# A two-layer encoder trunk in split fp32: embedding rows transposed inside the output projection, their products moved around the router, y split ahead of the next weights

## The reference

```python
x = x + merged @ w_o[i]
h2 = rms_norm(x, g_ffn[i])
logits = (t @ w_router).astype(jnp.float32)            # t = h2, 256 tokens, 8 experts
top_vals, top_idx = lax.top_k(logits, TOP_K)           # TOP_K = 2
w = jax.nn.softmax(top_vals, axis=-1)
...
acc = acc + g_e[:, None] * swiglu(t, wg_e, wu_e, wd_e) # for each expert e
x = x + acc
gate_p = jax.nn.sigmoid(rms_norm(x, g_ple[i]) @ w_ple_gate[i])
x = x + gate_p * (p[i] @ w_ple_up[i])                  # p[i]: 256 x 256
```

## Time and profile before

| | us |
|---|---|
| median of 3 runs | 1717.95 (1717.78 to 1718.05) |
| the profiled execution | 1716.82 |
| its span, first to last instruction | 1714.9 |
| TensorE matmuls busy | 1674.0 (98% of the span) |
| VectorE busy | 1334.2 (78%) |
| ScalarE busy | 1093.1 (64%) |

### The profile page before, as it was taken

One profiled execution on the slowest core, in us unless ns is written; L12 is line 12 of the kernel. 1 busy time (PEld: TensorE's weight loads), 2 busy tenths in 40 slices (PEclk: granted clock), 3 DMA queues, 4 the chain that ended last, 5 costly groups with the idle time before them and its releaser, 6 DMA issues.

```text
span 1714.9 us, 20962 instructions
## 1 busy us (share of the span) xinstructions
PE 1674.0 (98%) x7899; PEld 1389.7 (81%) x7899; DVE 1334.2 (78%) x1093; ACT 1093.1 (64%) x897; POOL 55.5 (3%) x52
## 2 busy tenths in 40 slices
PE   7999899999999998999999999999999999999997
PEld 6888788888778887888888888888888888888886
DVE  6785644545567856788988998999998999889885
ACT  5555344344455553777877877778778778778774
POOL 0100000000001000010000000000000000000000
PEclk9999999999999999899999999999999999999999
DMA  8433555565364335599999999999999999999990
GB/s 307 167 123 123 172 172 192 176 196 192 117 213 147 123 123 184 191 363 374 358 380 366 350 383 353 373 377 347 373 385 341 379 377 347 382 377 347 376 370 25
DMA packets 199549, 472.60 MB, mean 276 GB/s; under 512 B 8592, under 2 KB 11216, under 8 KB 199504
## 3 DMA queue, kind: packets, MB, share of 16 engines
q1 hardware_dynamic: 197936, 466.20, 75.6%
q0 software_dynamic: 1568, 5.77, 1.0%
HBM read 469.84 MB, written 2.10 MB: 275 GB/s over the span
## 4 chain that ended last, share of the span: by engine, by line
PE 86%; DVE 9%; issue 3%; ACT 2%; DMA 0%; SPq 0%; DVEq 0%; ACTq 0%
PE ps L1293 26%; PE ps L1295 26%; PE ps L1294 26%; DVE w_lo L786 5%; PE ps L1298 5%; PE ps L1622 1%; ACT w_hi L530 1%; DVE y_lo L1236 1%; DVE hT_lo L792 0%; ACT hT_hi L546 0%; PE ps L1542 0%; PE ps L1403 0%; ACT inner_hi L697 0%; DVE hT_lo L844 0%; PE ps L1384 0%
## 5 line engine op out<-in xcount | busy, mean ns | idle before, releaser
L786 DVE TENSOR_TENSOR w_lo<-raw,w_hi 128x2048 fp32r<-128x2048 f32 x442 | 1007.6, 2290 | 246.7 <-ACT w_hi L530 242.3
L530 ACT ACTIVATE w_hi<-raw 128x2048 fp32r<-128x2048 f32 x442 | 846.5, 1919 | 374.7 <-PE ps L1295 365.1
L1293 PE MATMUL ps<-w_hi,hT_hi 128*128 128x512 f32 (+1 forms) x1600 | 631.2, 394 | 10.9 <-DVE hT_lo L844 4.6
L1295 PE MATMUL ps<-w_hi,hT_lo 128*128 128x512 f32 (+1 forms) x1600 | 621.8, 389 | 0.0
L1294 PE MATMUL ps<-w_lo,hT_hi 128*128 128x512 f32 (+1 forms) x1600 | 621.2, 388 | 0.0
L1293 PEld LDWEIGHTS ps<-w_hi,hT_hi 128*128 128x128 f32 x1600 | 301.7, 189 | 77.3 <-DVE w_lo L786 6.0
L1295 PEld LDWEIGHTS ps<-w_hi,hT_lo 128*128 128x128 f32 x1600 | 301.4, 188 | 63.0
L1294 PEld LDWEIGHTS ps<-w_lo,hT_hi 128*128 128x128 f32 x1600 | 302.0, 189 | 58.8
L1293 PE MATMUL ps<-w_hi,inner_hi 128*128 128x512 f32 x608 | 240.3, 395 | 1.6 <-DVE inner_lo L792 1.6
L1295 PE MATMUL ps<-w_hi,inner_lo 128*128 128x512 f32 x608 | 237.8, 391 | 0.0
L1294 PE MATMUL ps<-w_lo,inner_hi 128*128 128x512 f32 x608 | 237.8, 391 | 0.0
(11 more groups left out here) (230 smaller groups left out, 776.2 us busy)
## 6 DMA issues: line engine op xcount, KB each, us to landing
raw<-in_w_moe_gate SPq DMA_DIRECT2D x112, 1024.0 KB, 6.9
raw<-in_w_moe_up SPq DMA_DIRECT2D x112, 1024.0 KB, 7.3
raw<-in_w_moe_down SPq DMA_DIRECT2D x112, 1024.0 KB, 6.7
raw<-in_w_in SPq DMA_DIRECT2D x38, 1024.0 KB, 5.6
raw<-in_w_dense_gate SPq DMA_DIRECT2D x14, 1024.0 KB, 5.0
raw<-in_w_dense_up SPq DMA_DIRECT2D x14, 1024.0 KB, 5.1
raw<-in_w_dense_down SPq DMA_DIRECT2D x14, 1024.0 KB, 4.8
raw<-in_w_o SPq DMA_DIRECT2D x8, 1024.0 KB, 4.8
```

Source lines behind the costliest of these rows:

```text
L530: nc.scalar.activation(w_hi[:, n % SLOTS, :], raw[:, n % RAW_SLOTS, :], ACT.Copy).then_inc(high_ready, 1)
L786: nc.vector.tensor_tensor(w_lo[:, n % SLOTS, :], raw[:, n % RAW_SLOTS, :], w_hi[:, n % SLOTS, :].bitcast(F32), ALU.subtract).then_inc(low_ ...
L1293: nc.tensor.matmul(o, x_parts[0][x_cols], parts[0], start=first, stop=False)
L1295: return nc.tensor.matmul(o, x_parts[1][x_cols], parts[0], start=False, stop=last)
```

## The change

The transposes of p for layer 1 move from in front of the router into the output projection, behind its second unit, and write bank 0 instead of bank 7. ScalarE's copy (`take_p`) and VectorE's `split_p` move with them. The whole first token tile of p @ `w_ple_up` is computed ahead of the router and the whole second tile between the router and the place counting; both write banks 4 to 7. The logits go to banks 0 and 1, the places to bank 2, so the router's first matmul now waits until banks 0 and 1 have been read. ScalarE's two copies of the products move forward, and its split of unit MOE + 2 stands ahead of the gathered tokens. VectorE splits unit MOE + 1 ahead of both gathered lows and unit MOE + 2 ahead of `extras`. In the item loop VectorE makes `y_lo` first and then splits units 1 and 2 of the next item, instead of unit 1, `y_lo`, and unit 2 in the next turn.

```diff
--- before.py
+++ after.py
@@ -143,7 +143,8 @@
 
     TASKS = [(0, 0, 8), (1, 0, 4), (1, 4, 4)]
     OUT_PRODUCTS = 5
-    P_BANK = [4, 7]
+    P_BANK = [4, 0]
+    LOGIT_BANK, PLACE_BANK = 0, 2
     OUT_BANK = [2, 2, 6]
     NORM_BANK = [0, 0, 4]
 
@@ -545,9 +546,7 @@
                         act_e.wait_ge(x_transposed, 4 * n + k // 2 + 1)
                     nc.scalar.activation(hT[0][:, k, :], banks(NORM_BANK[n % 3] + k // 2)[:, k % 2 * SEQ:(k % 2 + 1) * SEQ],
                                          ACT.Copy, scale=params[:, gain + k:gain + k + 1]).then_inc(hT_high, 1)
-                if n == 4:
-                    take_p(1)
-                else:
+                if n != 4:
                     keep_up(used, items, END if n == 5 else None)
                 for t in range(1 if n == 4 else 0, TILES):
                     nc.scalar.activation(normed[:, t, :], x[:, t, :], ACT.Square,
@@ -648,6 +647,9 @@
                     act_e.wait_ge(merged_transposed, 4 * layer + g + 1)
                     nc.scalar.activation(hT[0][:, 2 * g:2 * g + 2, :], banks(g).rearrange("p (k t) -> p k t", k=2),
                                          ACT.Copy).then_inc(mergedT_high, 1)
+                if layer:
+                    keep_up(base + WO_AT + 1)
+                    take_p(1)
                 keep_up(base + WO_AT + GATE_UNITS - 1)
 
             def dense():
@@ -669,9 +671,10 @@
                     act_e.wait_ge(ple_up_tile0, 1)
                 else:
                     act_e.wait_ge(units_used, UP1 + 1)
-                nc.scalar.activation(ple_up[:, t, :], banks(2 * t, 2), ACT.Copy).then_inc(ple_up_taken, 1)
+                nc.scalar.activation(ple_up[:, t, :], banks(4 + 2 * t, 2), ACT.Copy).then_inc(ple_up_taken, 1)
 
             def experts():
+                take_ple_up(0)
                 act_e.wait_ge(rstd_ready, 5)
                 for t in range(TILES):
                     act_e.wait_ge(x_gained_ready, t + 1)
@@ -680,15 +683,14 @@
                 act_e.wait_ge(top_ready, 1)
                 for t in range(TILES):
                     nc.scalar.activation(gate_w[:, t, :], gate_w[:, t, :], ACT.Exp, scale=rstd[:, t:t + 1]).then_inc(route_exps, 1)
-                take_ple_up(0)
+                take_ple_up(1)
+                keep_up(MOE)
 
                 for half in range(2):
                     act_e.wait_ge(gathered, half + 1)
                     nc.scalar.activation(hT[0][:, 4 * half:4 * half + 4, 0:P],
                                          banks(GATE + half).rearrange("p (k s) -> p k s", k=4),
                                          ACT.Copy).then_inc(gatheredT_high, 4)
-                take_ple_up(1)
-                keep_up(MOE)
                 act_e.wait_ge(counted, 1)
                 count = act_e.value_load(n_items_i[0:1, 0:1], min_val=EXPERTS, max_val=EXPERTS + EXTRA)
                 with act_e.Fori(0, count) as t:
@@ -1054,6 +1056,9 @@
                     dve.wait_ge(mergedT_high, 4 * layer + g + 1)
                     low(hT, banks(g).rearrange("p (k t) -> p k t", k=2),
                         (slice(None), slice(2 * g, 2 * g + 2))).then_inc(mergedT_ready, 1)
+                if layer:
+                    keep_up(base + WO_AT + 1)
+                    split_p(1)
                 keep_up(base + WO_AT + GATE_UNITS - 1)
                 add_to_x(4, 3 * layer + 1, base + WO_AT + GATE_UNITS)
 
@@ -1091,10 +1096,10 @@
                 e2 = [P, TILES, EXPERTS, EXPERTS]
                 dve.wait_ge(logits_done, 1)
                 for t in range(TILES):
-                    last = nc.vector.tensor_copy(logits[:, t, :], banks(GATE + t)[:, 0:EXPERTS])
+                    last = nc.vector.tensor_copy(logits[:, t, :], banks(LOGIT_BANK + t)[:, 0:EXPERTS])
                 link(last)
                 for t in range(TILES):
-                    last = nc.vector.tensor_tensor(logits[:, t, :], banks(GATE + t)[:, EXPERTS:2 * EXPERTS], logits[:, t, :], ALU.add)
+                    last = nc.vector.tensor_tensor(logits[:, t, :], banks(LOGIT_BANK + t)[:, EXPERTS:2 * EXPERTS], logits[:, t, :], ALU.add)
                 link(last)
                 other = logits[:, :, :].unsqueeze(2).to_broadcast(e2)
                 own = logits[:, :, :].unsqueeze(3).to_broadcast(e2)
@@ -1110,8 +1115,8 @@
                                         ALU.subtract).then_inc(top_ready, 1)
 
                 dve.wait_ge(places_done, 1)
-                place_ps = banks(TRA)[:, 0:TILES * EXPERTS].rearrange("p (t e) -> p t e", t=TILES)
-                count_ps = banks(TRA)[:, TILES * EXPERTS:(TILES + 1) * EXPERTS]
+                place_ps = banks(PLACE_BANK)[:, 0:TILES * EXPERTS].rearrange("p (t e) -> p t e", t=TILES)
+                count_ps = banks(PLACE_BANK)[:, TILES * EXPERTS:(TILES + 1) * EXPERTS]
                 link(nc.vector.scalar_tensor_tensor(place[:, :, :], place_ps, 1.0, chosen[:, :, :], ALU.add, ALU.mult))
                 link(nc.vector.tensor_scalar(item_place[:, :, 0:EXPERTS], place[:, :, :], -1.0, None, ALU.add))
 
@@ -1178,12 +1183,12 @@
 
             def experts():
                 route()
+                keep_up(UP1)
                 gathered_low(0)
-                keep_up(UP1)
                 gathered_low(1)
+                keep_up(MOE)
                 extras()
                 link(take_slots(slot_now, slice(0, 1)))
-                keep_up(MOE - 1)
                 count = dve.value_load(n_items_i[0:1, 0:1], min_val=EXPERTS, max_val=EXPERTS + EXTRA)
                 with dve.Fori(0, count) as t:
                     def actT_low_part(s):
@@ -1229,12 +1234,12 @@
                         dve.wait_ge(gatheredT_high, KD * (t + 1) + 4 * half + 4)
                         low(hT, banks(GATE + half).rearrange("p (k s) -> p k s", k=4),
                             (slice(None), slice(4 * half, 4 * half + 4), slice(0, P))).then_inc(gatheredT_ready, 1)
-                    keep_up(MOE + PER_ITEM - 1, t)
                     for half in range(2):
                         cols = slice(half * BANK, (half + 1) * BANK)
                         dve.wait_ge(item_y_high, t * 2 + half + 1)
                         nc.vector.tensor_tensor(y_lo[:, cols], banks(half), y_hi[:, cols].bitcast(F32),
                                                 ALU.subtract).then_inc(item_y_split, 1)
+                    keep_up(MOE + PER_ITEM, t)
                 for piece in range(4):
                     dve.wait_ge(item_combined, count * 4 + piece + 1)
                     xv = x[:, piece % 2, piece // 2 * BANK:(piece // 2 + 1) * BANK]
@@ -1278,7 +1283,6 @@
             mixer(1)
             gain_x(0)
             norm_low(4, FFN_GAIN + KD)
-            split_p(1)
             gain_x(1)
             embedding(1, experts())
 
@@ -1507,6 +1511,8 @@
                 for u in range(GATE_UNITS):
                     wide_unit(base + WO_AT, u, GATE_UNITS, hT, 4, ready=mergedT_ready, ready_at=4 * layer,
                               tile0_done=out_tile0 if u == GATE_UNITS - 1 else None)
+                    if layer and u == 1:
+                        flip_p(1)
 
             def dense():
                 def down(s):
@@ -1548,26 +1554,28 @@
 
                 for k in k_tiles:
                     for half in range(2):
-                        last = products(banks(2 * t + half), pT, columns(k, t), UP1, D, k, slice(half * BANK, (half + 1) * BANK),
+                        last = products(banks(4 + 2 * t + half), pT, columns(k, t), UP1, D, k, slice(half * BANK, (half + 1) * BANK),
                                         k == 0, k == PLE // P - 1)
                 if k == PLE // P - 1:
                     last.then_inc(ple_up_tile0 if t == 0 else units_used, 1)
 
             def route():
-                flip_p(1)
+                pe.wait_ge(x_updated, 8)
+                ple_up_tile(0)
                 for k in range(KD):
-                    if k % 2 == 0:
+                    if k == 0:
+                        pe.wait_ge(hT_ready, 16 + 2)
+                    elif k >= 4 and k % 2 == 0:
                         pe.wait_ge(hT_ready, 16 + k // 2 + 1)
                     for t in range(TILES):
 
-                        mm(banks(GATE + t)[:, 0:2 * EXPERTS], hT[0][columns(k, t)], router_parts[:, k, :, :], k == 0, False)
-                        last = mm(banks(GATE + t)[:, 0:EXPERTS], hT[1][columns(k, t)], router_parts[:, k, 0, :], False, k == KD - 1)
+                        mm(banks(LOGIT_BANK + t)[:, 0:2 * EXPERTS], hT[0][columns(k, t)], router_parts[:, k, :, :], k == 0, False)
+                        last = mm(banks(LOGIT_BANK + t)[:, 0:EXPERTS], hT[1][columns(k, t)], router_parts[:, k, 0, :], False, k == KD - 1)
                 last.then_inc(logits_done, 1)
-                pe.wait_ge(pT_ready, 2)
-                ple_up_tile(0)
+                ple_up_tile(1)
 
                 pe.wait_ge(chosen_ready, 1)
-                b = banks(TRA)
+                b = banks(PLACE_BANK)
```

(6 more changed lines are left out.)

## The result

The changed kernel takes 1726.22 us (median of 5 runs, 1725.31 to 1727.44) beside 1717.78 us of the kernel before on the same chip (5 runs, 1717.32 to 1718.05). The ratio is 1.0047 with a 95% interval of 1.0035 to 1.0058: slower, by 6.0 to 10.0 us. The forecast was 1726.1 in a range of 1720 to 1730. One run of a later kernel (after_filled) took 5584 us and is left out of that kernel's median. The profiled execution took 1725.31 us around a span of 1723.5; lines have moved by a few, so the products are now L1297, L1298 and L1299, `mm` is L1302, `y_lo` L1240, `w_lo` L788.

The account below looks back on a forecast made before the run. TensorE's matmuls, busy 98% of the span, were taken as the bound, so time moves only with its waits, clock or work. Terms -1.6 + 6.4 + 1.0 + 2.4 = +8.2 us gave median 1726.1, range 1720 to 1730.

Parts of the forecast that it names:

- Part 3: At item boundaries, y_lo first makes unit 1's split late: +0.82 each, 0.92 with later stops, +6.4 us over seven.
- The follow-up: Behind the late unit in each item, ScalarE's later split, table load and silu: 0.1 us taken, bounds 0 and 0.3.
- Rival 3: Boundary order costs nothing, the 0.38 goes at all seven; -3.3 to -6.5 us in all, about 1713; chance 0.08.
- Rival 4: A new wait of 0.5 us or more at every item's first transposes; +11.6 in all, 1729.5; chance 0.10.
- Parts 1 and 2: Transposes of p moved into the output projection (0.5 us cost), products and router reordered: -1.6 us together.
- Rival 1: The clock holds through the router: -4.8 in place of -1.6, +5.0 in all, 1723.0; chance 0.22.
- The clock: Granted clock low after TensorE's idle stretch behind the last item, slowing the last projection: +2.4 us, bounds 0 and 3.5.
- Part 4: Behind the last item: later adds to x (+1.0 us) and lower clock in the last projection (+2.4).
- The adds behind both splits: Behind the last item, VectorE's adds to x wait for both splits, so the last projection starts later: +1.0 us.
- Rival 2: The clock holds at both router and end: +2.6 or +1.9 in all, about 1720.3; chance 0.10.
- The sum: Whole kernel: -1.6 + 6.4 + 1.0 + 2.4 = +8.2 us, median 1726.1.
- the item term: The cost over seven item boundaries of splitting y ahead of the next weights: +6.4 us, bounds 5.7 and 7.8.

Follow-up runs that it names:

- after_filled: The changed kernel with unread 512-column matmuls ahead of both output projections and 17 behind the last spread matmuls: 1723.89 us, ratio 1.0033.
- experiment 1: The kernel before with one edit, y_lo ahead of the split of the next item's unit 1: 1723.59 us, ratio 1.0032.
- experiments 2 and 3: The changed kernel with unit 1 split ahead of y_lo again (1718.46 us), then with that split between the two halves of y_lo (1720.26 us).
- y_after_unit1: The changed kernel with unit 1 split ahead of y_lo again and unit 2 behind it in the same turn: 1718.46 us, ratio 1.0005.
- router_filled_again: Moved transposes, products and router with unread matmuls in TensorE's waits, old order of y and splits, timed again on one chip beside the filled kernel before: 1714.32 us.
- after_end_filled: The changed kernel with 17 unread 512-column matmuls behind the last item's spread matmuls: 1726.97 us, ratio 1.0050.
- transposes_alone: The kernel before with only the transposes of p, their copy and split moved into the output projection: 1717.9 us, ratio 0.9997.
- before_filled: The kernel before with unread matmuls around the transposes ahead of both output projections and 11 ahead of the last spread matmuls: 1711.33 us, ratio 0.9961.
- router_alone_filled: The changed kernel with the old order in item loop, extras and end, plus unread matmuls in TensorE's waits: 1715.48 us, ratio 0.9984.
- router_alone: The changed kernel with item loop, extras and end in the old order, leaving the moved transposes and products: 1718.94 us, ratio 1.0000.

## Why the prediction was right, point by point

- **Part 3, seven boundaries: +6.4 forecast, +7.24 measured.** The prediction has unit 1 "1.03 late, plus 0.17 for starting again", less 0.38 that unit 2 gives back: 0.82. Here unit 1 is 1.06 late (829.71 against 828.65), and the same sum gives 0.85. The follow-up was mis-sized: 0.1 was taken, about 0.2 is there. It stands at the sixth unit, which starts at 840.77 instead of 840.72 and whose 12 matmuls take 843.67 - 840.77 = 2.90 us and not 2.72. Rival 3, no cost at the boundary, is refuted by experiment 1. Its condition, that a delay costs only above about 0.5 us, is borne out by experiments 2 and 3: 0.6 late costs 0.15 per item, 1.5 late costs 1.04. Rival 4, a new wait of 0.5 or more at the first transposes, is not there: those waits are 0.3 at most, of weight loads.
- **Parts 1 and 2: -1.6 forecast, +0.6 - 2.05 = -1.45 measured.** The total is right, its make-up is not. Counted from the transposes of x, placing was forecast at 14.4 us and stands at 12.6 (695.17 - 682.57), since the clock fell at 692.1 and not near the router's end. The gather gives 1.7 of it back, 5.44 us against 3.73: "from the placing matmuls P the chain runs on as before" left out that the low level can reach it. Unit 3 of the first item starts at 30.3 us where 712.5 - 682.1 = 30.4 was forecast, behind a wait of 1.19 where about 1.0 was. Of the -2.05, the table makes 1.7 the clock's ((10.2 - 6.8) / 2) and 0.4 that of the split ahead of `extras`. So that the total agrees is luck: in y_after_unit1, with the same code up to here but 10.2 us at the low level, the two columns give +0.6 - 0.5 = +0.1. Rival 1, the clock held through the router, is half true and brings little, because the clock falls behind it. Its price was also added up wrongly: 693.6 + 16.0 is 709.6 and not 709.4, so that it should have been -4.5 and not -4.8.
- **The clock.** The row of the kernel before at 0.50 with TensorE busy all the time has its like here: from 692.00 to 694.00 the clock is 0.51 at a busy time of 2.00 of 2.00. The Trainium skill ("TensorE: Matmul & The Clock Gate", "HAM oscillation") speaks of idle gaps. The traces bear that out in part: ahead of and in layer 1's `w_o`, from 656 to 684 us, the clock is 1.00 in all five executions with fill there, while eight of the nine without it have 2.8 to 6.1 us at the low level in `w_o`. But in router_filled_again the level still falls inside the router, at 688.0, with TensorE busy 2.00 of 2.00 us in each window from 684 to 690. So in this kernel gaps are a cause and not the only one.
- **Part 4, the end: +3.4 forecast, +2.47 measured.** The adds behind both splits: +1.0 forecast; 10.99 us in after_end_filled, where the end runs at full clock, less 9.95 of the kernel before, is 1.04. The clock: +2.4 forecast, 41.18 - 39.76 = 1.4 measured. This term was mis-sized, since 14 products at the low level were assumed; the 16 transposes took half of the loss (3.32 against 2.58 us from their start to the first product), and only three or four products the rest. Both terms go by the profiled execution, whose own end had low clock in it; against 8.82 us, which transposes_alone and before_filled have there at full clock, the order costs 2.2 and the clock 0.3 more than it cost before. Rival 2, a full clock here too, did not come.
- **The sum.** -1.45 + 7.24 + 2.47 = +8.26, forecast +8.2. The errors of part 3 (+0.8) and part 4 (-0.9) cancel, which is luck as well. What is left of +8.60 does not come from the change: +1.78 ahead of `w_o`, from the start of the kernel, less 1.4 for the lower share of low clock in `w_o`.

The direction and the item term were foreseen for the right reason, and rivals 2, 3 and 4 are settled against. The 0.2% that a measurement was said to tell was about right, since 31 runs of one kernel spread over 8.8 us and a ratio's interval is 0.1 to 0.2% to either side.

## What to carry to other kernels

Before moving an instruction on an engine that works in order, count the spare time of what it is put ahead of: the price is small up to it, and above it is paid in each turn of the loop (1.0 us per item for one line here). Independent work moved from one wait to another gained nothing by itself here: the wait of 0.75 us went and one of 1.09 came where the work had stood. Where TensorE idles for a few microseconds among dense work, matmuls that nobody reads are worth a try, but time them in the order of work at hand: they brought 7.2 us with the old order and about 3.6 with the router's new one.

## What the runs showed that was not expected

- Fill in the idle stretches makes the kernel before faster by 0.43% (1710.7 against 1717.92 us), though it adds 39 matmuls. The runs are not clearly steadier for it: 12 runs of router_alone_filled spread over 9.6 us, 12 of router_alone over 8.6.
- The kernel before spreads from 1714.1 to 1722.91 us in 31 runs, and the time goes with the mean granted clock of the run (1714.1 at 0.995, 1717.92 at 0.992, 1722.28 at 0.988). The low stretches fall on other work in each execution, so single profiles of two kernels differ by up to 3.4 us in a stretch where their code costs the same; cutting the span in segments and taking off half of the low level's time leaves differences of some 0.2 us readable. This holds only where TensorE is busy throughout: behind the last item 5.3 us were at the low level, in part while TensorE waited, and half of it off 11.74 gives 9.1, where full clock gave 10.99 (after_end_filled).
- An item's time is steady to 0.02 us from one kernel to another (121.477 to 121.484 in seven kernels with the old loop, 122.519 to 122.543 in four with the new), so one profile settles the item term better than 31 timed runs.
